# Two expert stages on one core: the choice among three group sizes nested, with the 64-token case first

## The chip, the cores and the metric

The kernel runs on one core of a Trainium2 chip. The metric is the device time of one execution in microseconds; a kernel's time is the median of its runs.

## The reference

Two transformer blocks follow each other on 256 tokens of width 1024, all in float32. What matters here are their two mixtures of experts:

```python
def hier_moe(h, ...):            # first block: 16 experts, 2 per token, hidden width 512
    for e in range(MOE_EXPERTS):
        he = jax.nn.silu(h @ w_gate[e]) * (h @ w_up[e])
        out = out + combine[..., e:e + 1].astype(h.dtype) * (he @ w_down[e])

def expert_block(args):          # second block: 32 experts, 4 per token, hidden width 1024
    hb = xb @ w1[e] + b1[e]
    g = jnp.minimum(g, SWIGLU_LIMIT); u = jnp.clip(u, -SWIGLU_LIMIT, SWIGLU_LIMIT)
    return ((u + 1.0) * (g * jax.nn.sigmoid(g * SWIGLU_ALPHA))) @ w2[e] + b2[e]
```

How many tokens an expert gets is known only at run time, from the router's output. On average it is 32 in either stage.

## The kernel before

Everything outside the expert stages is straight-line code with an order written out by hand; semaphores tie the engines together. Each engine runs its own program.

An expert's tokens are gathered with a matmul against a 0/1 matrix (`pick`), go through gate, up and down projections, and are scattered back with the transposed matrix. The group's size is one of three, held per expert in `sizes`: code 0 for at most 64 tokens (`H2`), 1 for at most 128 (`P`), 2 for all 256 (`T`). The program holds a body of instructions for each size, and `by_size` (lines 381 to 385) chooses: it tests `size == c` for c = 0, 1, 2 in turn, with a body behind each test. The test is line 384. An engine whose size is 0 runs the first body, then meets two more tests, each of which jumps over a body.

TensorE (`experts`, from line 1716) goes through `by_size` 7 times for an expert of the first stage and 11 times for one of the second. In the second stage the order is: gate and up of the first half (`half_up`, line 1616, bias line 1621), `scatter` of the expert before (line 1689), gate and up of the second half, `turn_hidden` (1634), `gather` of the next expert (1671), `turn_hidden`, two `half_down` (1652 for size 0, 1655 for size 1), and `turn_picks` (1702 for size 0, 1704 for size 1). Ahead of each expert three sizes are read into registers (`size_of`, line 375). The loop on TensorE holds `PASS` = 4 experts, so that the first stage makes 4 trips and the second 8; its closing branch is on line 1763 and carries a hint for the branch (`hint_back_edge`, line 379). `rows_of` (682), `turned` (689) and `outputs_and_picks` (695) are ScalarE's copies; VectorE's part is `picks` (1173), `hidden2` (1336 to 1345) and `add_outputs` (1188). ScalarE goes through `by_size` twice for an expert, once inside the other; VectorE once.

Counted in the code with its float32 matmuls (two weight loads and two matmuls for each call, half of that for a transpose), one trip of TensorE's second expert loop is 5,091 instructions long, and one of the first 2,790. All three bodies are in that count; a trip in which every expert has size 0 executes less than half of it and jumps over the rest. A choice in `half_up` of the second stage is 72 instructions for size 0, 36 for size 1 and 72 for size 2, with three tests; in `half_down` 32, 32 and 64; in `gather` 64, 64 and 1; in `turn_picks` 16, 4 and 4. From the loop's head to the first instruction of the first gate body there are 17.

SyncE loads the weights, 2 MB a piece, into a ring of 6 slots (line 463 in the first stage, 503 in the second). It has no size choices.

Of the kernel before, what the change touches and what calls it, by code (L numbers as in the profile page):

```python
# [11 lines left out]
P = 128  # L12
T = 256
# [17 lines left out]
def build(nc, a):  # L31
# [11 lines left out]
    with ctx:  # L43
# [327 lines left out]
        H2 = P // 2  # L371
# [8 lines left out]

        def by_size(eng, size, body):

            for c, w in enumerate((H2, P, T)):
                with eng.If(size == c):
                    body(w)


        @block.sync
# [178 lines left out]
        def _(act):  # L567
# [131 lines left out]

            act.wait_ge(sem("gathered1"), 1)  # L700
            by_size(act, size_of(act, 0), rows_of(1, 0))
            with looped(act, 0, n1_exp) as e:
                size, size_next = size_of(act, e), size_of(act, e + 1)

                def body(w):
                    act.wait_ge(PD, 3 * e + (n_s1 + 1))
                    act.wait_ge(sem("sg_free"), e + 1)
                    s.activation(SG[:, 0:4 * w], ps[0][:, 0:4 * w], ACT.Silu).then_inc(gate_free, 1)
                    turned(1, 0, e, w)
                    by_size(act, size_next, rows_of(1, e + 1))  # L710
                    outputs_and_picks(1, e, w, 3 * e + (n_s1 + 3))

                by_size(act, size, body)
# [1190 lines left out]
```

## Time and profile before

| | us |
|---|---|
| median of 3 runs | 2508.3 (2503.12 to 2519.26) |
| profiled execution, its time | 2512.87 |
| its span in the trace | 2511.1 |
| first expert stage | about 400 to 719 |
| second expert stage | about 1331 to 2492 |

The page of the profile gives each engine's busy time and its share of the span. A matmul's records stand on PE, its weight loads on PEld; tests, register loads and branches of an engine's sequencer are not counted as busy, but the views of a single line list them with their durations. The chain that ended last is followed backwards from the end of the program; "issue" in it is time in which an engine waited for nothing that the profile shows.

### The profile page before, as it was taken

How to read it: one execution, taken by the hardware profiler on the slowest of the kernel's cores; microseconds unless marked ns; L12 is line 12 of the kernel's file. 1: busy time of each engine (PE TensorE's matmuls, PEld its weight loads, DVE VectorE, ACT ScalarE, POOL GpSimd, SP SyncE). 2: the span in 40 equal slices, each digit the busy share in tenths (PEclk: the TensorE clock that was granted, in tenths of full speed). 3: DMA queues.
4: the chain of work that ended last, by engine and by line, in shares of the span. 5: the costliest groups of instructions: out<-in, count | busy, mean ns of one | idle time of the engine just before them, and what ended most of it. 6: DMA issues, size and time to landing. Idle time of an engine off the chain costs nothing.

```text
span 2511.1 us, 32392 instructions
## 1 busy us (share of the span) xinstructions
PE 2247.6 (90%) x12228; PEld 1328.1 (53%) x12229; DVE 589.5 (23%) x1216; ACT 370.2 (15%) x718; POOL 6.5 (0%) x23
## 2 busy tenths in 40 slices
PE   7969877889998997788858999899999999999996
PEld 5655445556545686633335554445455555555553
DVE  2352512211222015500031212111221222222113
ACT  1032101121111014300011111101011111111111
POOL 1000000000000000000000000000000000000000
PEclk9989997999999976588877989999998999999998
DMA  8822253998966340022225999859799999999990
GB/s 289 317 101 82 86 201 120 327 356 312 325 224 233 102 150 19 1 100 100 100 78 198 393 363 345 312 202 380 270 386 381 339 393 376 393 383 393 384 370 18
DMA packets 272763, 621.67 MB, mean 248 GB/s; under 512 B 12200, under 2 KB 19026, under 8 KB 272510
## 3 DMA queue, kind: packets, MB, share of 16 engines
q1 hardware_dynamic: 272302, 616.95, 67.1%
q8 instruction: 241, 3.95, 0.6%
q10 hardware_dynamic: 208, 0.67, 0.1%
q14 instruction: 12, 0.10, 0.0%
HBM read 616.55 MB, written 1.05 MB: 246 GB/s over the span
## 4 chain that ended last, share of the span: by engine, by line
PE 87%; DVE 6%; issue 4%; ACT 3%; POOL 0%; ACTq 0%; DVEq 0%; POOLq 0%
PE pair L1616 26%; PE pair L1410 16%; PE pair L1652 10%; PE pair L1671 8%; PE pair L1397 6%; PE pair L1689 4%; PE pair L1621 3%; PE pair L1655 2%; PE pair L1459 2%; PE pair L1451 1%; PE pair L1825 1%; PE pair L1434 1%; PE pair L1422 1%; PE pair L1702 1%; PE pair L1414 1%
## 5 line engine op out<-in xcount | busy, mean ns | idle before, releaser
L1616 PE MATMUL pair<-ring,r_at 128*64 128x256 f32 (+1 forms) x4864 | 662.0, 402 | 53.2 <-issue 49.5
L1616 PEld LDWEIGHTS pair<-ring,r_at 128*64 128x64 f32 (+1 forms) x4864 | 385.6, 143 | 317.2 <-issue 177.2
L1652 PE MATMUL pair<-ring,r_big 128*64 128x512 f32 x1152 | 263.9, 609 | 0.0
L1410 PE MATMUL pair<-ring,x_T 128*128 128x512 f32 (+1 forms) x608 | 236.9, 545 | 2.5 <-ACT r_big L719 1.1
L1671 PE MATMUL pair<-r_big,r_mix 128*128 128x64 f32 (+1 forms) x1600 | 204.3, 290 | 23.1 <-DVE r_big L1338 11.4
L1671 PEld LDWEIGHTS pair<-r_big,r_mix 128*128 128x128 f32 x1600 | 197.8, 205 | 34.0 <-issue 33.2
L1173 DVE TENSOR_SCALAR r_big<-iota,rank 128x128 f32<-128x128 f32 x100 | 24.1, 283 | 752.0 <-PE pair L1621 577.0
L1410 PEld LDWEIGHTS pair<-ring,x_T 128*128 128x128 f32 x608 | 107.5, 190 | 125.0 <-issue 123.0
L1652 PEld LDWEIGHTS pair<-ring,r_big 128*64 128x64 f32 x1152 | 80.4, 140 | 151.2 <-issue 149.9
L1397 PE MATMUL pair<-x_T,ring 128*128 128x256 f32 x656 | 152.8, 391 | 7.8 <-DVEq L838 6.4
L1397 PEld LDWEIGHTS pair<-x_T,ring 128*128 128x128 f32 x656 | 125.9, 195 | 32.3 <-issue 8.0
L1689 PE MATMUL pair<-r_at,r_big 64*128 64x512 f32 (+1 forms) x400 | 106.2, 614 | 7.0 <-issue 5.7
L1188 DVE SCALAR_TENSOR_TENSOR r_big<-pair,combine,r_big 128x512 f32<-128x512 f32 x132 | 90.0, 744 | 47.4 <-PE pair L1689 46.9
L813 ACT ACTIVATE r_big<-r_big 128x256 f32<-128x256 f32 (+1 forms) x64 | 28.3, 443 | 445.0 <-DVE r_big L1336 445.0
L1621 PE MATMUL pair<-r_big,ones 1*64 1x256 f32 (+1 forms) x480 | 90.4, 416 | 0.0
L1410 PE MATMUL pair<-ring,r_big 128*128 128x512 f32 x144 | 76.3, 691 | 13.2 <-DVE r_big L1288 5.2
L1338 DVE TENSOR_SCALAR r_big<-pair 128x256 f32<-128x256 f32 (+1 forms) x64 | 29.3, 458 | 231.5 <-PE pair L1621 231.5
L695 ACT COPY r_at<-pair 128x512 f32<-128x512 f32 (+1 forms) x48 | 29.8, 621 | 284.0 <-PE pair L1652 231.0
L1459 PE MATMUL pair<-r_big,r_at 128*128 128x64 f32 (+2 forms) x272 | 50.4, 354 | 20.4 <-ACT r_at L614 20.4
L1689 PEld LDWEIGHTS pair<-r_at,r_big 64*128 64x128 f32 (+1 forms) x400 | 37.6, 186 | 54.9 <-issue 54.9
L682 ACT COPY r_at<-pair 128x512 f32<-128x512 f32 (+1 forms) x50 | 31.0, 619 | 229.4 <-PE pair L1671 229.4
L689 ACT COPY r_big<-pair 128x256 f32<-128x256 f32 (+1 forms) x80 | 31.5, 394 | 220.7 <-PE pair L1634 220.6
(310 smaller groups left out, 1602.7 us busy)
## 6 DMA issues: line engine op xcount, KB each, us to landing
ring<-exp_w SPq DMA_DIRECT2D x192, 2048.0 KB, 12.5
ring<-w_in SPq DMA_DIRECT2D x24, 2048.0 KB, 9.2
ring<-w_gate SPq DMA_DIRECT2D x16, 2048.0 KB, 11.4
ring<-w_up SPq DMA_DIRECT2D x16, 2048.0 KB, 13.4
ring<-w_down SPq DMA_DIRECT2D x16, 2048.0 KB, 9.2
ring<-mod_w SPq DMA_DIRECT2D x12, 2048.0 KB, 13.5
ring<-w_out SPq DMA_DIRECT2D x4, 2048.0 KB, 8.0
ring<-w_branch SPq DMA_DIRECT2D x3, 2048.0 KB, 7.6
```

The costliest lines, as they stand in the source:

```text
L682: s.copy(XG[:, :, 0:n], got[:, :, 0:n]).then_inc(sem(f"xg_ready{b}"), 1)
L689: s.copy(HIDT[:, half, 0:4 * w], ps[2 - b][:, 0:4 * w]).then_inc(sem(f"hiddenT_ready{b}"), 1)
L1188: ins = v.scalar_tensor_tensor(out=dst[:, t, 512 * h:512 * h + 512], in0=ps[2 + t][:, 512 * h:512 * h + 512], scalar=comb0[:, t, bass.ds(e ...
L1397: ins = mm(out[:, ct], w[:, k, c0 + P * ct:c0 + P * ct + P], xT[:, k], start=(k == 0), stop=(k == nk - 1 and bias is None))
L1410: ins = mm(out[:, t, 0:n], xT[:, k, P * t:P * t + P], w[:, k, c0:c0 + n], start=(k == 0), stop=(k == nk - 1 and bias is None))
L1459: ins = mm(ps[3][:, 512 * (c % 2) + w * h:512 * (c % 2) + w * h + w], PT[0:rows, c % 2, h * nt + kt], map_values(kind, 4 * hc + h, kt), st ...
L1616: ins = mm(out, stat(k), w_[:, k, c0:c0 + n], start=(k == 0), stop=(bias is None and k == KD - 1))
L1621: ins = mm(out, ones[32 * q:32 * q + 1, 0:rows], b1q[32 * q:32 * q + 1, buf, c0:c0 + n], start=False, stop=True)
L1652: ins = mm(ps[2][H2 * h:H2 * h + H2, 0:512], hT[:, at:at + H2], cols, start=beg, stop=end)
L1655: ins = mm(ps[2 + t][:, 512 * h:512 * h + 512], hT[:, 512 * t + P * f:512 * t + P * f + P], cols, start=beg, stop=end)
L1671: ins = mm(ps[b - 1][:, P * k:P * k + w], HT[:, t, P * k:P * k + P], pick[:, buf, t, 0:w], start=(t == 0), stop=(t == NT - 1))
L1689: ins = mm(ps[2 + t][:, 512 * h:512 * h + 512], pickT[r, P * t:P * t + P], y, start=True, stop=True)
```

## The change

`by_size` tests for size 0 first, with the other two cases inside its `Else`, where size 1 is tested and size 2 is the second `Else`.

```diff
         def by_size(eng, size, body):
 
-            for c, w in enumerate((H2, P, T)):
-                with eng.If(size == c):
-                    body(w)
+            with eng.If(size == 0):
+                body(H2)
+            with eng.Else():
+                with eng.If(size == 1):
+                    body(P)
+                with eng.Else():
+                    body(T)
```

The bodies, their order in the program, the waits and the data are the same.

## Rows read from the trace of the kernel before

**Rows 1.** The page: span, busy time of the engines

```profile
span 2511.1 us, 32392 instructions
...
PE 2247.6 (90%) x12228; PEld 1328.1 (53%) x12229; DVE 589.5 (23%) x1216; ACT 370.2 (15%) x718; POOL 6.5 (0%) x23
```

**Rows 2.** Chain that ended last, 2039.2 to 2070.1: start us, us, what

```profile
2039.53 3.45 PE pair L1616 x32
2042.99 0.58 PE pair L1621 x4
...
2053.84 3.60 PE pair L1616 x32
```

**Rows 3.** The same chain over the loop's end, 2058 to 2083.5

```profile
2069.74 0.44 PE pair L1702 x8
2070.18 4.38 issue
2074.55 2.00 PE pair L1616 x9
2076.55 0.90 issue
2077.45 4.93 PE pair L1616 x23
```

**Rows 4.** Line 384's tests, whole span: ns min/median/max, first and last start

```profile
L384 PEldq COMPARE_BRANCH  x1404: 68/214/3359, 400.2 to 2488.6; - x176
L384 ACTq COMPARE_BRANCH  x294: 43/91/104, 408.3 to 2486.1; - x147
L384 DVEq COMPARE_BRANCH  x144: 102/115/139, 419.1 to 2468.6; - x144
```

**Rows 5.** TensorE's tests at four moments, and the loop's branch behind one

```profile
L384 PEldq COMPARE_BRANCH  x2: 214/214/214, 2036.4 to 2036.6; - x2
...
L384 PEldq COMPARE_BRANCH  x1: 353/353/353, 2041.1 to 2041.1; - x1
...
L384 PEldq COMPARE_BRANCH  x1: 2654/2654/2654, 2063.0 to 2063.0; - x1
...
L1763 PEldq COMPARE_BRANCH  x1: 3952/3952/3952, 2067.7 to 2067.7; - x1
```

**Rows 6.** The loop's branch in all 12 trips, and once at 1934.9

```profile
L1763 PEldq COMPARE_BRANCH  x12: 85/3816/5454, 479.1 to 2479.3; - x12
...
L1763 PEldq COMPARE_BRANCH  x1: 457/457/457, 1934.9 to 1934.9; - x1
```

**Rows 7.** DMA queues (packets, MB, share): whole span, then 2071.6 to 2202.8

```profile
q8 instruction: 241, 3.95, 0.6%
...
q8 instruction: 21, 0.34, 1.1%
```

**Rows 8.** Chain over the loop's end behind an expert of size 1

```profile
1792.64 13.74 PE pair L1655 x32
...
1806.59 3.60 PE pair L1616 x32
```

**Rows 9.** Who waited for whom, 1338 to 2490: us in total, times, longest

```profile
DVE r_big L1173 <- PE pair L1621: 577.0, 32, 27.2
ACT r_big L813 <- DVE r_big L1336: 445.0, 64, 16.0
...
PE pair L1616 <- issue: 30.0, 15, 5.2
```

**Rows 10.** Chain in the first expert stage, over a loop's end, 470 to 505

```profile
481.49 5.69 issue
```

**Rows 11.** Windows: us, PE, PEld, DVE, ACT, POOL, PEclk, DMA share, GB/s

```profile
2075.00:2082.00 7.00, 6.10 (x29) 4.16 (x26) 0.00 (x0) 0.00 (x0) 0.00 (x0) 0.51 1.02 404
2082.00:2122.00 40.00, 39.37 (x299) 21.69 (x298) 10.56 (x23) 4.72 (x9) 0.00 (x0) 1.00 0.99 366
```

## Prediction

> **What bounds the kernel now.** I read the page first, then the chain that ended last in both expert stages, then the sequencer's own records of lines 384, 375 and 1763, then the instruction queue among the DMA queues. TensorE is busy for 90% of the span, the next engine for 23% [rows 1]. In the second expert stage the chain lies on TensorE almost without a break: an expert of size 0 takes from 2039.53 to 2070.18, 30.65 us [rows 2, 3]. The others wait for it: VectorE's `picks` 577 us in all, ScalarE's sigmoid 445 us [rows 9]. So tests on VectorE (115 ns) and ScalarE (91 ns, rows 4) lie under TensorE's work; taking some away is worth nothing.
>
> What TensorE loses in that stage is not work: 30.0 us before line 1616 for which no releaser is shown [rows 9]. It sits at the loop's end: after `turn_picks` TensorE stands still for 4.38 us, runs 9 matmuls, and stands still for 0.90 us more [rows 3]. The sequencer's records say why. The loop's branch took 3.95 us [rows 5], and has a median of 3.8 us over 12 trips [rows 6]. Tests of line 384 cost 214 ns as a rule but reach 3.36 us [rows 4]. The long ones are few and far between, and the instruction queue moves 241 packets, 16 KB each (3.95 MB / 241) [rows 7]; 21 of them fall in one trip. A trip has 5,091 instructions, so a packet is some 256 of them (5,091 / 256 = 19.9 packets, touching 20 or 21). I read a long test as a jump that lands in a packet not yet there.
>
> The spacing of these stalls is the number that all hangs on. One test starts at 2063.0 and lasts 2.65, so its packet came at 2065.6; the loop's branch starts at 2067.7 and lasts 3.95, so the next came at 2071.6 [rows 5]. That is 6.0 us from entering one packet to having the next. Behind it TensorE starved again at matmul 9 until 2077.45 [rows 3]: 5.9 us after 2071.6. So the sequencer gets one packet per 6.0 us at best, and an expert of 30.65 us spans 5,091 / 4 / 256 = 5.0 packets, 29.8 us. Fetching and TensorE's work are nearly level. What keeps fetching hidden is how far the sequencer runs ahead: after `turn_picks` was issued its next test began at 2036.4 [rows 5], while TensorE reached the next gate at 2039.53 [rows 2], 3.1 us ahead; after a gate body, 2041.1 against 2043.57, 2.4 us ahead. Whether a wait shows depends on where a packet's edge falls.
>
> **The change, part by part.** *Time of the tests.* Size 0 now meets one test and one jump instead of three tests, of which two are taken. A taken one costs 214 ns [rows 4] and some 60 ns to the next. If the new jump costs nothing, 0.55 us are saved per choice, if it costs as much as a taken test, 0.27. No row shows an unconditional jump; I take the latter. The sequencer does this while TensorE works through its queue, 2.4 to 3.1 us deep, so it is worth nothing on the chain but for what follows a stall. The Trainium skill (Advanced Engine Details and Errata, Control Flow Timing) gives about 51 ns for a branch that is always taken and 108 ns for a compare-and-branch. This trace's 214 ns for a taken one is twice that; by the page the saving would be nearer 0.5 us per choice, hidden just the same.
>
> *Length of the code.* Before, each body falls into the next test, so a choice costs three tests. Nested, it costs two tests and two jumps: the first body must jump over both others, the second over the third. That is one instruction more per choice: 44 in a trip of the second loop (5,135), 28 in one of the first (2,818). As packets that is little: 0.17 of one, 1 us of fetching per trip. But it moves the edges.
>
> *Where the edges fall.* Matmul 9 of the first gate is its instruction 18 [rows 3]; with the 17 ahead of it an edge lies 35 instructions behind the loop's head. The branch is at 5,091 - 35 = 5,056 = 19 x 256 + 192, so 192 instructions into its packet. That agrees with the 2.1 us from entering it (2065.6) to the branch (2067.7). Ahead of the second loop stand 1 + 28 + 1 + 1 = 31 choices' worth of shift, so the head comes to 4 instructions before an edge, or onto the edge if it is placed there. From the edge, 5,135 = 20 x 256 + 15: the branch is 15 instructions into a packet. Counting on from there, the five edges of an expert now lie in up of the first half, gate and up of the second half, at the end of the first `half_down`, and in `turn_picks`. Before, the last one fell into the next gate's body, where TensorE had 9 to 22 matmuls to go on with.
>
> *What that costs.* Let s be the start of an expert's first gate; its work ends at s + 30.65 [rows 2, 3]. The second gate ends at s + 14.3; the sequencer enters the packet behind it 2.4 us sooner, at s + 11.9. Each packet takes 6.0: up at 17.9, `half_down` at 23.9, `turn_picks` at 29.9. From there it still has to read three sizes and test: from the branch's end at 2071.6 to the first matmul at 2074.55 [rows 3, 5] that took 2.9 us; without the loop's own part 2.6. The next gate starts at s + 32.5, 1.9 us late. There are 22 such places (28 experts of size 0, less 6 that end a trip): 42 us. At a trip's end comes one packet more: 29.9 + 6.0 + 2.9 = 38.8, a gap of 8.2 where it was 4.38 + 0.90 = 5.3: 2.9 us, 6 times, 17 us. Where an expert of size 1 ends the trip the gap was hidden by 13.74 us of down matmuls [rows 8]; its `turn_picks` was issued some 5.6 us early (13 matmuls of 0.43), now 6.0 + 2.9 - 5.6 = 3 us show. Back come about 3 us where stalls had delayed the first `gather` of a trip. In the first stage, counted back from the same edge, the branch moves from 107 to 136 instructions into its packet; its last packet is then entered about a test earlier. Of the 5.69 us there [rows 10], between nothing and 2 come back; I take 1, three times, 3 us.
>
> Sum, against the profiled execution of 2512.9: + 42 + 17 + 3 - 3 - 3 = + 56, so 2569. That execution was 4.6 above the median of the runs, so 2564.
>
> *The clock.* After the gap of 5.3 us the granted clock was 0.51, close to the lower of its two levels, 1.2 GHz, for 7 us, then 1.00 [rows 11]; the 23 matmuls took 4.93 us instead of 2.6. If each new gap of 1.9 us did that, 22 x 2.3 = 51 us came on top. No row shows a gap of 1.9 us and what follows it; I take none of it into the sum and keep it for the range.
>
> **The rivals.** *The head stays 4 instructions before an edge* (12%). Then each of the 7 returns waits for a second packet with nothing to run: 7 x 6.0 = 42 us more, 2606.
>
> *Fetching stays as hidden as it is* (26%): the added instruction isn't there, or the edges land as kindly as now. Then only the saved 0.27 us per choice remains, where the sequencer is behind: some 1 to 1.5 us at 10 returns. That gives 2493 to 2508. For it: fetching is hidden in most of a trip now. Against it: the jump over two bodies must be somewhere. The Trainium skill (Runtime: NRT & Kernel Launch, Instruction fetch mechanics) says that crossing a block is mostly hidden, and also that a taken branch out of the window stalls; by its first half this rival would win, and the stalls of several us in this trace agree with its second.
>
> *Faster* (12%): the edges fall so that the loop's last packet is entered early. It happened once: at 1934.9 the branch took 0.46 us [rows 6]. With that at all 10 returns, each loses 4 to 5 us of its gap, 40 to 50 us, 2460 to 2468. It decides where 5.5 us of TensorE's work lie between entering the last packet and the branch. By my count there are under 0.5.
>
> **How the numbers follow.** The forecast has 50%. The predicted time is its own, 2564; its own range is 2535 (1.0 us a place, no clock) to 2615 (all of the clock). The range over all reaches from 2488, which takes in the rival without effect and leaves out most of the faster one, to 2630, the second packet with half the clock's cost. About 1% is what a measurement of this kernel can tell from no change, with runs from 2503 to 2519. Slower by over 1%: 50 + 12 = 62%. Within 1%: 26%. Faster: 12%.
>
> **What would show it.** Right: in the chain of the second stage, a gap of about 2 us ahead of the first gate of most experts, of about 8 at a trip's end, and no gap behind matmul 9; the loop's branch at 5 to 6 us; some 500 tests on TensorE in place of 1,404. Stalls of 6.0 us spacing, but gaps elsewhere: the count of instructions is wrong. No stall at all behind the tests: the reading of the packets is wrong. Experts that each take 30.65 us or less, with the gaps at the trips' ends as before, would make it wrong altogether.

## The result, and the profile after

| | before | after |
|---|---|---|
| median | 2505.7 us (2501.23 to 2519.26, 4 runs) | 2580.95 us (2577.61 to 2593.57, 4 runs) |
| ratio to before, 95% interval | | 1.0302 (1.0257 to 1.0347) |
| time of the profiled execution | 2512.9 us | 2593.6 us |
| first expert stage, first gate to the last gap | 303.6 us | 300.6 us |
| second expert stage, first gather to the last gap | 1155.6 us | 1235.2 us |

The nested kernel is 75 us, 3.0%, slower. Its lines stand four further down: gate and up are on line 1620 (bias 1625), `half_down` on 1656, `turn_picks` on 1706, `gather` on 1675, `scatter` on 1693 and the loop's branch on 1767. The test for size 0 is now line 383, the one for size 1 line 386.

The page of after, span and busy times. It answers to [rows 1]:

```profile
span 2591.7 us, 31832 instructions
...
PE 2261.4 (87%) x12228; PEld 1334.8 (52%) x12229; DVE 589.6 (23%) x1216; ACT 366.2 (14%) x716; POOL 6.5 (0%) x23
```

The same work is done; TensorE's busy time is 14 us longer, the span 81.

Who waited for whom in after, TensorE, 1338 to 2580 (us in total, times, longest):

```profile
PE pair L1620 <- issue: 100.2, 27, 9.2
PE pair L1675 <- DVE r_big L1342: 9.1, 30, 0.6
```

The first line is the 30.0 us of [rows 9], grown to 100.2.

The chain that ended last in after, over one expert's start, a whole expert and its end (start us, us, what):

```profile
1373.86 0.44 PE pair L1706 x8
1374.30 2.27 issue
1376.56 3.67 PE pair L1620 x32
...
1406.93 0.44 PE pair L1706 x8
1407.37 2.31 issue
```

The same chain in the fifth trip, with two gaps within it and the one at its end:

```profile
2042.13 0.44 PE pair L1706 x8
2042.57 2.37 issue
2044.93 5.36 PE pair L1620 x32
...
2077.51 2.42 issue
2079.93 3.67 PE pair L1620 x32
...
2110.93 8.59 issue
```

A gap of some 2.3 us (1.9 to 2.6) stands ahead of the first gate of 21 experts, with `turn_picks` (L1706) directly before it; in [rows 2] and [rows 3] an expert followed the other without one. At six trips' ends it is 8.2 to 9.2 us, and behind it the 32 gate matmuls run through without the second break of [rows 3]. The six of them add up to 51.9 us, the 21 to 48.3 us, together the 100.2 of the line above.

TensorE's tests in after, at the three moments of this chain in which one was long, then the loop's branch and all tests (ns min/median/max, first and last start):

```profile
L383 PEldq COMPARE_BRANCH  x1: 3035/3035/3035, 1371.1 to 1371.1; - x1
...
L383 PEldq COMPARE_BRANCH  x1: 2072/2072/2072, 1392.8 to 1392.8; - x1
...
L383 PEldq COMPARE_BRANCH  x1: 2975/2975/2975, 1404.2 to 1404.2; - x1
...
L1767 PEldq COMPARE_BRANCH  x1: 5509/5509/5509, 2111.1 to 2111.1; - x1
...
L383 PEldq COMPARE_BRANCH  x892: 73/183/3280, 404.5 to 2568.4; - x179
L386 PEldq COMPARE_BRANCH  x88: 67/125/337, 1540.5 to 2569.1; - x88
```

Each long test is a jump into a packet not yet there. The trace also has the instruction queue's transfers one by one, and they bear this out: in the 14 profiled runs of this case, from the first expert stage on, TensorE's sequencer has 793 tests, jumps and loop branches of over 1 us, and every one of them ends 1.3 to 1.55 us after a packet has landed. In the stretch shown, packets land at 1372.7, 1393.5, 1399.5 and 1405.7. With those 1.4 us the sequencer has them at 1374.2 (1371.1 + 3.04), at 1394.9, at some 1401 (no long test stands there) and at 1407.2. The last of these is the packet behind the fifth edge of the expert: it lies in `turn_picks`, whose matmuls end at 1407.4, 0.2 us after the packet is there. The next matmul starts at 1409.69, 2.5 us after it. There are 980 records where [rows 4] has 1,404. A jump is recorded as a compare-and-branch too: 892 are 468 tests and 424 jumps, 88 are 44 and 44. Test and jump alternate for an expert of size 0, so they can be told apart: a test that falls through has a median of 75 ns, the jump behind the body one of 188 ns.

### The profile page after: what moved, and what is told of

It is laid out like the page before. It is cut to its first block, busy times and chain, and to the rows that moved or that the text cites. A ratio compares the mean times of both kernels' runs of the same rounds, so it can differ in the third digit from the quotient of the medians.

```text
span 2591.7 us, 31832 instructions
## 1 busy us (share of the span) xinstructions
PE 2261.4 (87%) x12228; PEld 1334.8 (52%) x12229; DVE 589.6 (23%) x1216; ACT 366.2 (14%) x716; POOL 6.5 (0%) x23
## 4 chain that ended last, share of the span: by engine, by line
PE 85%; issue 6%; DVE 5%; ACT 3%; POOL 0%; ACTq 0%; DVEq 0%; POOLq 0%
PE pair L1620 26%; PE pair L1414 16%; PE pair L1656 10%; PE pair L1675 8%; PE pair L1401 6%; PE pair L1693 4%; PE pair L1625 3%; PE pair L1659 2%; PE pair L1463 2%; PE pair L1455 1%; PE pair L1829 1%; PE pair L1438 1%; PE pair L1426 1%; PE pair L1706 1%; PE pair L1418 1%
## 5 line engine op out<-in xcount | busy, mean ns | idle before, releaser
L1620 PE MATMUL pair<-ring,r_at 128*64 128x256 f32 (+1 forms) x4864 | 678.6, 412 | 124.3 <-issue 120.2
L1620 PEld LDWEIGHTS pair<-ring,r_at 128*64 128x64 f32 (+1 forms) x4864 | 392.6, 147 | 401.3 <-issue 269.2
L1656 PE MATMUL pair<-ring,r_big 128*64 128x512 f32 x1152 | 258.7, 599 | 0.0
L699 ACT COPY r_at<-pair 128x512 f32<-128x512 f32 (+1 forms) x48 | 29.8, 622 | 281.7 <-PE pair L1656 227.4
L1463 PEld LDWEIGHTS pair<-r_big,r_at 128*128 128x128 f32 (+1 forms) x272 | 48.5, 272 | 29.2 <-ACT r_at L618 29.2
```

Source lines behind the costliest of these rows:

```text
L699: s.copy(YS[:, 0:n], ps[2][:, 0:n]).then_inc(sem(f"ys_ready{b}"), 1)
L1463: ins = mm(ps[3][:, 512 * (c % 2) + w * h:512 * (c % 2) + w * h + w], PT[0:rows, c % 2, h * nt + kt], map_values(kind, 4 * hc + h, kt), st ...
L1620: ins = mm(out, stat(k), w_[:, k, c0:c0 + n], start=(k == 0), stop=(bias is None and k == KD - 1))
L1656: ins = mm(ps[2][H2 * h:H2 * h + H2, 0:512], hT[:, at:at + H2], cols, start=beg, stop=end)
```

## The experiments

The theory: TensorE's sequencer gets a packet of code (some 256 instructions) at best every 6.0 us. ("At best" is a little too strong: the 167 spacings between packets in after's second stage have a median of 6.2 us, but 23 are under 5.8 and one is 3.2.) A choice is one instruction longer, so the edges and the loop's branch stand elsewhere, and the stalls show where TensorE has nothing queued. The rival: the tests and jumps themselves cost the time, on TensorE or on the other engines. A second rival: the place matters, but for another reason than the arrival of code.

**1. Nested on TensorE alone**

```diff
-            with eng.If(size == 0):
+            if eng is nc.tensor:
+                ...                       # nested
+            else:
+                for c, w in enumerate((H2, P, T)):
+                    with eng.If(size == c):
+                        body(w)
```

> The nested choice on TensorE alone; ScalarE and VectorE keep their three tests in a row. Theory (packet edges of TensorE's code): all of the loss is here, 2570 to 2595 us, ratio about 1.03 to the kernel before, with gaps of 2.3 us ahead of the gates and 8.6 at the trips' ends. Rival (the nested code on ScalarE or VectorE delays a copy or a mask): within 1% of 2506 us.

Measured: 2591.1 us, ratio 1.0332 (1.0305 to 1.0359). The whole loss is there, and so are the gaps: 97.6 us ahead of the gates.

**2. Nested on ScalarE and VectorE alone** (the condition of the first turned round)

> The nested choice on ScalarE and VectorE alone; TensorE keeps three tests. Theory (packet edges of TensorE's code): no change, 2500 to 2512 us. Rival (the nested code on ScalarE or VectorE): 2550 us or more.

Measured: 2517.1 us, 5 above the range expected, ratio 1.0029 (1.0004 to 1.0054). Fewer tests on those two engines bring nothing, as their waits of hundreds of us [rows 9] let expect. The loss is TensorE's.

**3. All nested, with the head of TensorE's second loop put on place 221 of a packet.** That is where it stood before by the count of the prediction (an edge 35 instructions behind it).

```diff
-            return nc.Fori(start, end, engines=[eng.engine], hint_back_edge=True)
+            return nc.Fori(start, end, engines=[eng.engine], hint_back_edge=True,
+                           head_slot=None if slot is None else {eng.engine: slot})
...
-                with looped(pe, 0, n // PASS) as i:
+                with looped(pe, 0, n // PASS, {1: None, 2: 221}[b]) as i:
```

> The changed kernel with one thing more: the head of TensorE's second expert loop is placed 221 instructions into a packet of 256, which is where the count puts it in the kernel before (35 ahead of an edge). Same tests and jumps as in the changed kernel. Theory (where the edges fall): the loss is gone, 2485 to 2510 us, no gaps ahead of the gates but at the trips' ends 4 to 6 us. Rival (a jump over two bodies is dear wherever it stands): stays at 2560 to 2590 us.

Measured: 2505.7 us, ratio 0.9984 (0.9956 to 1.0013), level with the kernel before. Every test and every jump of the change is still in it. The profile's waits of TensorE over the same stretch:

```profile
PE pair L1621 <- issue: 22.5, 12, 4.2
```

and the chain of it over a trip's end:

```profile
1472.92 0.44 PE pair L1707 x8
1473.36 3.08 issue
1476.44 2.17 PE pair L1621 x9
1478.60 0.73 issue
```

The gaps within the trips are gone and the break behind matmul 9 of [rows 3] is back at its place. So the tests and jumps aren't the price, their effect on places is.

**4. The kernel before, nothing nested, with the head on place 16** (the same edit, 16)

> The kernel before, three tests in a row on all engines, with the head of TensorE's second expert loop placed 16 instructions into a packet, so that an edge falls into the picks' turn or the reading of the sizes of three experts in each trip of four. Theory (where the edges fall): slower though nothing is nested, 2540 to 2585 us, with gaps of about 2 us ahead of three gates a trip and nearly none at the trip's end. Rival (nesting itself costs): 2500 to 2512 us.

Measured: 2546.8 us, ratio 1.0168 (1.0144 to 1.0193): about half of the loss can be had without any nesting. Its waits:

```profile
PE pair L1617 <- issue: 43.6, 28, 2.7
```

Most experts now have a gap ahead of the gate, while at the trips' ends, where the loop's branch took 0.5 to 2.0 us, it is 0.9 to 2.5 us, less than before. So the gaps within a trip and those at its end, two terms of the prediction's sum, move apart from each other.

**5. Nested, head on place 184**

> The nested kernel with the head of TensorE's second expert loop set on place 184 of a packet of 256 instructions (two packets' worth of places lie between the edge of the kernel after and this one; with 221, the place of the kernel before, the loss was gone). Theory: TensorE's sequencer gets a packet of code at most every 6.0 us, and what is lost depends on where in a packet the back edge and the 64-token paths fall. With 184 the branch stands at 184 + 5,135 = 20 x 256 + 199, so it is well inside its packet when it runs: no loss comes back. Worked with the packet time of 6.0 us: 5 to 10 us under the nested kernel with 221 (2,505.7), so 2,495 to 2,502. Rival (only the very place 221 is good, for another reason than packets): 2,520 to 2,580.

Measured: 2493.9 us, ratio 0.9951 (0.992 to 0.9982). Faster than both kernels by a small but real amount, just under the range expected. Its only gaps over 2 us ahead of a gate are the six at trips' ends, 4.0 to 4.2 us.

**6. Nested, the 256-token bodies left out of TensorE's second loop** (this part of the computation is missing; no expert of this input has size 2)

```diff
+            if cut256[0]:                 # set on TensorE's second loop only
+                with eng.If(size == 0):
+                    body(H2)
+                with eng.Else():
+                    body(P)
+                return
             with eng.If(size == 0):
```

> The nested kernel with the 256-token bodies left out of TensorE's second expert loop, which no expert of this input runs: with two sizes left, each choice there is one test with an else. The loop falls from 5,135 to some 3,300 instructions, 13 packets a trip in place of 21, its head stays where the compiler put it. Theory (fetch of code): 13 packets at 6.0 us are 78 us against some 128 us of work in a trip, so the gaps of 2.3 us ahead of the first multiplication of an expert go for the most part, and only the one at the loop's end stays; the loss against the kernel before is gone: 2,470 to 2,520. Rival (running the tests and the jumps of 180 to 210 ns is what costs): a 64-token choice keeps its one test and its jump, so the time stays near the nested kernel's, 2,560 to 2,590.

Measured: 2477.1 us, ratio 0.9881 (0.9837 to 0.9925). An expert of size 0 runs the same instructions as in after; only the code that it jumps over is shorter, and 104 us against after are gone. The profile has, first in the queues of the page and then in TensorE's waits of the second stage:

```profile
q8 instruction: 178, 2.92, 0.5%
```

```profile
PE pair L1628 <- DMA ring<-exp_w: 6.4, 8, 1.3
PE pair L1628 <- issue: 4.0, 8, 0.7
```

242 packets in after, 178 here: 64 fewer in 8 trips, 8 a trip, from 21 to 13. Thirteen at 6.0 us are 78 us in a trip of four experts, 122.6 us by [rows 2, 3], and the gaps ahead of the gate fall from 100.2 to 4.0 us. The packets now follow each other at a median of 10.1 us, so fetching is no longer at its limit. What TensorE waits for most ahead of a gate is a weight load, 6.4 us in all; its largest wait in the stage is 11.4 us for VectorE ahead of `gather`, the same as in before.

**7. The kernel before with the same bodies left out**

> The kernel before with the same 256-token bodies left out of TensorE's second expert loop: two tests in a row at each choice there. Theory (fetch): the small gaps go, the one at the loop's end stays or halves: 2,465 to 2,505, and within 25 us of the nested kernel cut in the same way, the sign depending on where the loop's head falls in a packet. Rival (tests and jumps): 10 to 20 us faster than before for a third of the tests gone, and some 75 us faster than the nested kernel cut in the same way.

Measured: 2485.6 us, ratio 0.9916 (0.9891 to 0.9941), 8 us above the nested kernel cut likewise, with intervals that overlap; in the two profiles the stage is equally long (1123.1 and 1122.8 us from the first gather to the last matmul ahead of the final scatter). With less code the two forms are near each other, where the rival wanted 75 us between them. The branch at the trip's end took 1.6 us here and 0.5 us in the sixth, and the gaps ahead of the gate add up to 21.8 us: where the head falls still shows in the gaps.

**8. The kernel before, head on place 44**

> The kernel before, nothing nested, with the head of TensorE's second loop on place 44 of a packet. Theory: on place 16 it took 41 us more than on its own place, 221; the 64-token paths of the four experts now cross packet edges 28 places earlier in the code. Worked with 6.0 us a packet: some 30 us more than before, so 2,530 to 2,550, less than on place 16. Rival (the place acts only by the first packet's filling, the less of it is left the longer the stall at the loop's end): at least as slow as on place 16 or no slower than before.

Measured: 2576.1 us, ratio 1.0289 (1.025 to 1.0328), twice the loss expected. Its waits and its chain over a trip's end:

```profile
PE pair L1617 <- issue: 80.9, 27, 9.0
```

```profile
2064.38 2.23 issue
2066.61 5.36 PE pair L1617 x32
...
2099.29 8.97 issue
```

These are after's gaps, and for the same reason: 44 + 5,091 = 5,135, so the branch stands 15 instructions into its packet, just as from head 0 with 5,135. The kernel before, with its three tests in a row, can be made as slow as the nested one by place alone. Of the loss of some 66 us, 51 are gaps (80.9 less the 30.0 of [rows 9]) and 11 are longer matmuls (1120.6 us of TensorE's busy time in the stage against 1110.0), which the expected 30 us had no place for. The rival had forecast a time at least as long as on place 16, and that came true, so this time doesn't speak against it. The table behind experiment 12 does: it wants the longest gap at a trip's end where the least of the head's packet is left, and the gap is 4.7 to 5.3 us with 35 instructions left (before, 221), but 6.7 to 9.0 with 212 (44).

**9. Nested, head on place 0**

> The nested kernel with the head of TensorE's second loop set on place 0 of a packet, the edge itself. If the compiler had already moved the head of the nested kernel onto the edge, as one of the two readings of the prediction has it, this is the nested kernel again: 2,575 to 2,590, with gaps of 2.3 us ahead of the first multiplication of an expert within a trip and 8.6 us at the trips' ends. If the head had stayed 4 instructions before the edge, the two differ, and this one should be off by more than 5 us.

Measured: 2588.8 us, ratio 1.0314 (1.0271 to 1.0357), and TensorE's waits are after's:

```profile
PE pair L1621 <- issue: 100.1, 27, 8.9
```

So after's head stood on the edge already. The medians alone wouldn't say so: they lie 8 us apart, though the ratios to before (1.0302 and 1.0314) agree within their intervals. What decides are the 27 gaps, and the records behind the loop's branch: had an edge stood 4 instructions behind the head, the sequencer would break off between two reads of a size there. In after it runs from the branch's end at 2116.57 to the first gate at 2119.52 without such a break, while the next packet lands only at 2120.4, behind all 17 instructions of the head. Experiment 11 shows what such a break looks like.

**10. Nested, head on place 104**

> The nested kernel with the head on place 104. Theory (packets at 6.0 us): the branch stands at 104 + 5,135, place 119 of its packet; worked as for place 184, about the same time: 2,485 to 2,505, while place 44 of the kernel before lost 66 us. Rival (the early half of a packet is bad for a head as such, 0, 16 and 44 all lost time): 2,530 to 2,590.

Measured: 2489.0 us, ratio 0.9907 (0.9874 to 0.9939), the lowest time of a whole kernel here: 23 us faster than before, 92 faster than after. The early half of a packet isn't bad as such. Waits and chain over a trip's end:

```profile
PE pair L1621 <- issue: 30.0, 6, 5.6
```

```profile
2048.36 0.44 PE pair L1707 x8
2048.80 5.56 issue
2054.37 5.35 PE pair L1621 x32
...
2086.41 0.44 PE pair L1707 x8
2086.85 3.45 PE pair L1621 x32
```

It loses as much to gaps as before (30.0 us), yet it is faster; the windows below show by what.

**11. The sixth without the hint on the second loop's back edge**

```diff
-                with looped(pe, 0, n // PASS) as i:
+                with looped(pe, 0, n // PASS, b == 1) as i:     # hint_back_edge
```

> The nested kernel with the 256-token bodies left out of TensorE's second loop, as before, and without the hint on that loop's back edge, which asks for the head's code ahead of the branch. Theory: with 13 packets a trip there is time to fetch ahead and no gap was left at the trips' ends; without the hint the head is asked for only as the branch runs, so a gap of some 4 to 6 us comes back at each of the 7 trips' ends: 25 to 45 us more than with the hint (2,477.1), 2,500 to 2,525. Rival (the gap at a trip's end has nothing to do with fetching the head): no change, 2,470 to 2,485.

Measured: 2548.5 us, ratio 1.0147 (1.0121 to 1.0173), 71 us above the sixth. TensorE's waits in that stage:

```profile
PE pair L1628 <- issue: 71.0, 7, 11.5
```

Without the hint six of the seven returns have a gap of 11.1 to 11.5 us, and the one behind an expert of size 1 has 3.7. The expectation had 4 to 6 for each. The sequencer's records show two packets in the place of one, here for the return at 1942.5 (the loop's branch, then the first and the second read of a size):

```profile
L1776 PEldq COMPARE_BRANCH  x1: 6269/6269/6269, 1942.5 to 1942.5; - x1
...
L375 PEldq TENSOR_LOAD <-sizes x1: 302/302/302, 1949.0 to 1949.0; - x1
...
L375 PEldq TENSOR_LOAD <-sizes x1: 307/307/307, 1954.7 to 1954.7; - x1
```

The branch takes 6.3 us, where it took 0.5 in the sixth: that is the head's packet, which lands at 1947.4. Then five instructions run, up to 1949.7, and the sequencer stands for 5.0 us until the next packet, landed at 1953.2. The same break of 4.7 to 5.0 us is there at all seven returns and at none of the sixth. So here the head stands 5 instructions ahead of an edge. That is the case of the prediction's first rival (4 instructions, a second packet at each return), and this is what it would have cost. The 71 us aren't the price of the hint alone, then; some 5 of each 11 belong to the second packet. Whether the hint would have hidden that one too, and where the sixth's head stands, isn't shown.

**12. The kernel before, head on place 104**

> The kernel before, nothing nested, with the head of TensorE's second loop on place 104, where the nested kernel took 2,489 us, 23 less than before. Theory A (the place is all there is): the rows kernel gains as much there, 2,485 to 2,500. Theory B (length of code and time of the tests matter too, since fetching and TensorE's work are nearly level): three tests in a row take some 0.27 us more a choice behind each late packet and the loop is 44 instructions shorter, which puts the edges elsewhere; worked with 6.0 us a packet, 5 to 15 us slower than before, so 2,515 to 2,530.

Measured: 2519.0 us, ratio 1.0028 (1.0001 to 1.0055), 30 us above the nested kernel with the same head place, as the second of the two theories had it. Why is shown in part only. In the profiles the stage is 27 us longer than in experiment 10: gaps ahead of the gates make 10 of it (39.6 against 30.0), others ahead of `half_down` 4, and the same matmuls take 1103.3 us against 1089.4. And with the same head place the two branches stand 75 and 119 instructions into their packets, so the edges differ as well. At 221 the two forms were level (experiment 3). Which form is the better one apart from its places isn't shown.

The places side by side. "Branch" is the loop's branch in its packet: head place + length (5,091 or 5,135), less whole packets of 256. The places of the heads of before and after and the two lengths come from the count of instructions. Where the first gate of a trip has two breaks, both are in the gap.

| kernel | head | branch | gap at a trip's end, us | gaps ahead of the gate in all, us | us |
|---|---|---|---|---|---|
| after | 0 | 15 | 8.2 to 9.2 | 100.2 | 2581 |
| before's form (8) | 44 | 15 | 6.7 to 9.0 | 80.9 | 2576 |
| before's form (12) | 104 | 75 | 6.0 to 6.8 | 39.6 | 2519 |
| nested (10) | 104 | 119 | 5.5 to 5.7, once 2.2 | 30.0 | 2489 |
| before | 221 | 192 | 4.7 to 5.3, once 2.7 | 30.0 | 2506 |
| nested (5) | 184 | 199 | 4.0 to 4.2 | 26.1 | 2494 |
| nested (3) | 221 | 236 | 2.4 to 4.8 | 22.5 | 2506 |
| before's form (4) | 16 | 243 | 0.9 to 2.5 | 43.6 | 2547 |

Two things move. The further the branch stands in its packet, the earlier that packet was entered, and the smaller the gap at the trip's end, by and large. Within a trip gaps are there at nearly every expert for heads on 0, 16 and 44 and nearly nowhere for 104, 184 and 221: an expert is almost exactly 5 packets long (5,135 / 4 / 256 = 5.01), so the edges fall at the same spot of every expert, good or bad for all.

Gaps aren't all. Windows of the second stage, from the first gather to the last gap, have the columns us, busy time of PE, PEld, DVE, ACT and POOL, granted clock, DMA share, GB/s. Before, after and nested with head 104, one fence each:

```profile
1331.60:2487.20 1155.60, 1109.96 (x7032) 605.56 (x7032) 220.05 (x448) 144.57 (x257) 0.00 (x0) 0.96 0.92 340
```

```profile
1332.60:2567.80 1235.20, 1122.09 (x7032) 608.67 (x7032) 220.06 (x448) 142.81 (x257) 0.00 (x0) 0.95 0.87 318
```

```profile
1328.30:2462.50 1134.20, 1089.42 (x7032) 591.22 (x7032) 220.07 (x448) 142.21 (x257) 0.00 (x0) 0.98 0.93 347
```

The same 7,032 matmuls take 1110, 1122 and 1089 us, at a mean granted clock of 0.96, 0.95 and 0.98. That is how the tenth beats before with equal gaps: 20.5 us less of matmul time.

## Why the prediction was right, and where its sum was short

**The mechanism** stood: packets at 6.0 us, a head on the edge (experiment 9, and the records of experiment 11, against the rival with 12%), a branch 15 instructions into its packet with 5 to 6 us (5.5 in the record above), a fifth edge in `turn_picks`, gaps of about 2 and about 8 us, nothing behind matmul 9. The rival without effect and the faster one both needed edges that fell otherwise. Experiment 3 shows what the first looks like; no place tried came near the faster one's 2460 to 2468 us. One term of the sum was right in size only, by luck: that of the first stage, below.

**Gaps within a trip**: 22 x 1.9 = 42 us forecast, 21 with a mean of 2.3, 48.3 us measured. Per expert: packet in `turn_picks` at s + 29.9 by the sum, at s + 30.6 by the trace (1407.2 - 1376.6). The one in up of the second half came at s + 18.3 and not 17.9, so 0.4 us lie ahead of it, and the two that followed took 12.3 us together, 6.15 each (they land at 1399.5 and 1405.7). Reading sizes and the test took 2.5 us, not 2.6.

**Trip's end**: 5.3 to 8.2 was the sum, 8.2 to 9.2 the trace. Six gaps make 51.9 us, where all of before's came to 30.0 [rows 9]: + 22 against + 17. Both ends of the sum were a little off: the mean is 8.6 in after, and 4.6 in before, since its six are 4.7 to 5.3 and once 2.7 (27.6 in all; the other 2.4 of the 30.0 are small gaps elsewhere).

**Size 1 ending a trip**: + 3 forecast, nothing there. At 1830.4 the gate follows the down matmuls of 13.74 us without a gap, as in [rows 8]: the loop's branch there takes 2.65 us and ends at 1826.2, so that the sequencer was ready some 1 us before those matmuls ended.

**First gather of a trip**: - 3 forecast, - 3.5 measured (waits for VectorE and issue ahead of `gather`).

**First stage**: - 3 forecast, - 3.0 measured, and this is luck. The forecast had each of the three returns give back 1 us. Their gaps are 5.69, 5.75 and 4.90 us in before and 5.68, 4.92 and 5.49 in after, 16.3 and 16.1 in all. The 3.0 came from elsewhere: 2.1 from small gaps ahead of `scatter` and `gather`, 1.5 from shorter matmuls (280.0 us against 278.5). The other gaps ahead of gates grew by 0.8.

**The clock** was the largest single miss, and it was left out of the sum knowingly. Windows of after, behind the gap of 2.37 us:

```profile
2045.00:2048.40 3.40, 3.40 (x18) 2.05 (x20) 0.00 (x0) 0.90 (x1) 0.00 (x0) 0.50 1.00 380
2048.40:2077.40 29.00, 28.73 (x214) 15.84 (x210) 6.61 (x14) 2.43 (x6) 0.00 (x0) 1.00 0.98 355
```

TensorE stood for 2.37 us, then the granted clock was 0.50, the lower level of 1.2 GHz, for at least 3.4 us, and the gate's 32 matmuls took 5.36 us; after that it was 1.00. Behind the gap of 2.42 us at 2077.51 they took 3.67 us at a granted clock of 1.00. Of the 18 gaps within trips that an expert of size 0 follows, 10 have gate matmuls of 5.2 to 5.4 us behind them and 8 have 3.67; what tells them apart isn't shown. Nor is it shown that the gap alone brings the clock down: the kernel before has 6.8 us at 0.50 from 1494.7, with no gap over 0.6 us in the 20 us ahead of them. The price over the stage is 12 us of busy time (1109.96 to 1122.09), about a quarter of the 51 us kept for the range. All together on the profiled pair: 70.2 for the gaps, 12.1 for the matmuls and 3.5 back make 79 of the stage's 79.6 us. Less 3.0 for the first stage, that is + 76, with the clock in it, where the sum said + 56 without it. The profiled pair differs by 80.7 us, since the part ahead of the first expert stage, which has no choices, ended 4.4 us later; the medians differ by 75.

**The tests** bring nothing, as forecast. A size-0 choice has one test and one jump, and the two of [rows 4]'s kind that went were hidden. The jump's price had no row in before; it is 188 ns, so the value taken (as a taken test, 214) was near.

## What to carry to other kernels

Where an engine's loop is so long that its code is fetched anew in each trip, and runs only a part of it, count code against time: here 1,284 instructions in 30.65 us were at the limit of one packet in 6.0 us, and one instruction more at each of 44 choices, or the head's place alone, decided over 3% of the kernel. Before judging an edit of such a loop by its time, run it with the head on two or three places; else the place is measured, not the edit (at place 104 the same edit gains 1.2%, at 221 it changes nothing that can be told from noise, at its own it loses 3.0%). The sounder cure is less code: bodies that never ran cost eight packets a trip. Taking away the back edge's hint cost 71 us where fetching had time to run ahead, a good part of it because the head then stood 5 instructions ahead of an edge. With the hint, 8.6 us a trip were still left where the branch stood 15 instructions into its packet.

## What the runs showed of the hardware that was not expected

A jump to the end of a choice is recorded like a compare-and-branch and costs 188 ns (median) where a test that falls through costs 75. Every long test, jump or loop branch of TensorE's sequencer, 793 of them, ends 1.3 to 1.55 us after a packet of code has landed. A loop without its hint, with its head 5 instructions ahead of an edge, waits for two packets at a return, some 11 us, where the expectation had one. A loop head that came to 4 instructions before an edge by the count stood on the edge. Behind 10 of 18 gaps of some 2.3 us the gate matmuls took 5.2 to 5.4 us in place of 3.67; behind the one shown the granted clock was 0.50 for 3.4 us.
